# One-hot rows of a routing matrix, built by two engines in place of one

## The chip, the cores and the metric

The kernel runs on one core of a Trainium2 chip. The metric is the device time of one execution in microseconds (us). The profiler's record of one execution is the source of every row shown here; its engines are PE (TensorE matmuls), PEld (its weight loads), DVE (VectorE), ACT (ScalarE), POOL (GpSimd) and SP (SyncE, which issues the weight stream's transfers). A "q" behind an engine's name marks its instruction queue.

## The reference, cut to what matters

One layer of a streaming encoder is computed for 640 tokens: projections, two attentions, a merge, and then PEER, a product-key lookup over 128 x 128 experts. Only PEER touches the change:

```python
v1, i1 = lax.top_k(s1, PEER_TOPK)
v2, i2 = lax.top_k(s2, PEER_TOPK)
...
experts = e1 * PEER_KEYS + e2
gate = jax.nn.softmax(sc, axis=-1)
...
act = jax.nn.gelu(jnp.einsum('nhkd,nd->nhk', u, xt))
w = (gate * act).astype(xt.dtype)
return jnp.einsum('nhk,nhkd->nd', w, v)
```

Each token has 128 picks (8 heads x 16), each with a first key e1, a second key e2 and a gate.

## The kernel before

For 384 of the 640 tokens the kernel doesn't gather expert rows. It computes all 128 x 128 expert activations densely, and multiplies them with a gate matrix G[e1, e2] of each token. G is a product of two 128 x 128 matrices of a token, both with one row per pick: `oh1` has the gate at column e1, `oh2` has a 1 at column e2. So each token costs VectorE two rows-tiles and TensorE one 128 x 128 x 128 product.

The stage that makes G is three loops that run beside each other, one per engine. Each has six trips (the variable `i`) of 16 sets (the variable `q`), and a set is four tokens, so there are 96 sets. In this text set n is the n-th of them, from 0.

- TensorE (L679 to L693) runs two k-steps of an expert unit (L639, six matmuls of 384 columns), waits for `oh_ready` and for `g_evac`, and then makes the four products of the set (L691) into one of two PSUM banks.
- VectorE (L1393 to L1402) waits until the products of the set two before are done (`g_full`), and makes the set's eight tiles, two `tensor_scalar` for each token: L1399 for `oh2`, L1400 for `oh1` with its gate. There are two sets of buffers.
- ScalarE (L1001 to L1014) waits for the products, and copies the bank into a staging buffer (L1007, the evacuation). After sets 7 and 15 of a trip it issues a store of 2 MB to DRAM (L1011), in 512-byte pieces. After the evacuations of sets 8 and 15 it also applies Gelu to an expert unit (L978) and issues a store of that unit (L980). Everything stands in one in-order queue.
- GpSimd splits the next unit's fp32 weights into a high and a low part as soon as TensorE is done with a unit, which is once in 8 sets: one `tensor_scalar` of 2048 columns (L362) and four `tensor_tensor` of 512 (L366). Ten such bursts fall into the 96 sets: the last trip has none.

The rows of the set are `fp32` in SBUF. `iota` is a constant tile with 0 to 127 in each row, `pick_t[0]`, `[1]` and `[2]` hold gate, e1 and e2 with one column per token. Behind the stage ScalarE waits for its stores, and a long stage of expert groups follows.

Of the kernel before, what the change touches and what calls it, by code (L numbers as in the profile page):

```python
# [6 lines left out]
P = 128  # L7
# [12 lines left out]
PH, TOPK, KEYS = 8, 16, 128  # L20
# [6 lines left out]
GT = 32  # L27
GBLK = N2 // GT
# [83 lines left out]
def build(nc, x_t, wstream, u_rows, v_rows, cka, cva, ckb, cvb, rext, negs, bp_b, bs_b, sinks, lnp, lnrow, subk, consts, pt_out, y_out, n_out):  # L112
    f32, f32r, u32 = mybir.dt.float32, mybir.dt.float32r, mybir.dt.uint32
    ALU, ACT = mybir.AluOpType, mybir.ActivationFunctionType
    AX = mybir.AxisListType
    ds = bass.ds

    with ExitStack() as ctx:
# [6 lines left out]
        def sem(name):  # L125
            return ctx.enter_context(nc.semaphore(name))
# [29 lines left out]
        ident, ones, iota, bmask = (cst[:, P * i:P * i + P] for i in range(4))  # L156
# [34 lines left out]
        pick_t = [W2[:, N2 * (q + 2):N2 * (q + 3)] for q in range(3)]  # L191
        oh1 = W2[:, 5 * N2:5 * N2 + 8 * P].rearrange("p (n e) -> p n e", n=8)
# [8 lines left out]
        oh2 = m1_hi[:, 2 * EG * N2:2 * EG * N2 + 8 * P].rearrange("p (n e) -> p n e", n=8)  # L201
# [24 lines left out]
        def acc(s, h):  # L226

            return banks[:, 2 * s + h, 0:WAVES[h][1]]

        def cut(ap, h):  # L230

            return ap[:, WAVES[h][0]:WAVES[h][0] + WAVES[h][1]]
# [11 lines left out]
        def sc_parts(s):  # L244

            return banks[:, 4 + 2 * s, :], banks[:, 5 + 2 * s, 0:P]
# [34 lines left out]
        gexp_in, gexp_done, picks_done, picks_full, picks_taken = (  # L281
            sem(n) for n in ("gexp_in", "gexp_done", "picks_done", "picks_full", "picks_taken"))

        oh_ready, g_full, g_evac = sem("oh_ready"), sem("g_full"), sem("g_evac")
        act_stored = [sem(f"act_stored{s}") for s in range(2)]
        act_in = [sem(f"act_in{e}") for e in range(EG)]
# [163 lines left out]
        def _(pe):  # L450
# [4 lines left out]
            def k_step(s, k, dst, k_first, k_last, phase):  # L455

                if phase is not None and k % 2 == 0:
                    pe.wait_ge(mv_ready, KT_N * phase + k + 2)
                for n, (a, b) in enumerate(((w_hi, mv_hi), (w_hi, mv_lo), (w_lo, mv_hi))):
                    for h in range(2):  # L460
                        last = pe.matmul(acc(dst, h), a[s][:, P * k:P * k + P], b[h][:, k, :],  # L461
                                         start=(k == k_first and n == 0), stop=(k == k_last and n == 2))
                return last
# [121 lines left out]
            with pe.Fori(0, N_PROJ // 2) as i:  # L585
                for s in range(2):
                    m = 2 * i + s
                    pe.wait_ge(split_done, U_PROJ + m + 1)
                    for z in range(2):
                        pe.wait_ge(z_taken, 2 * m + z + 1)  # L590
                        for k in range(8 * z, 8 * z + 8):
                            last = k_step(s, k, z, 8 * z, 8 * z + 7, 1)
# [32 lines left out]
            with pe.Fori(0, N_QUERY // 2) as i:  # L625
# [3 lines left out]
                for k in range(KT_N):  # L629
                    last = k_step(1, k, 1, 0, KT_N - 1, 3)  # L630
# [5 lines left out]
            def act_step(s, k, bank):  # L636

                for n, (a, b) in enumerate(((w_hi, mv_hi), (w_hi, mv_lo), (w_lo, mv_hi))):
                    last = pe.matmul(banks[:, bank, 0:N2], a[s][:, P * k:P * k + P], b[1][:, k, :],  # L639
                                     start=(k == 0 and n == 0), stop=(k == KT_N - 1 and n == 2))  # L640
                if k == KT_N - 1:
                    last.then_inc(unit_done, 1)
                return last
# [23 lines left out]
            for q, src in enumerate((pick_g, pick_e[0], pick_e[1])):  # L667
                for b in range(N2 // P):
                    last = pe.transpose(banks[:, 4 + q, P * b:P * b + P], src[:, 2 + b, :], ident)
# [9 lines left out]
            with pe.Fori(0, GBLK // 2) as i:  # L679
                for q in range(2 * GT // 4):  # L680
                    for k in (2 * q, 2 * q + 1):
                        s, n = k // KT_N, TAIL + 2 * i + k // KT_N
                        if k % KT_N == 0:
                            pe.wait_ge(split_done, U_PEER + n + 1)
                            pe.wait_ge(gelu_done, n - 1)
                        act_step(s, k % KT_N, s)
                    pe.wait_ge(oh_ready, 16 * i + q + 1)
                    pe.wait_ge(g_evac, 16 * i + q + 1)
                    for t in range(4):
                        n = 4 * (q % 2) + t  # L690
                        last = pe.matmul(banks[:, 2 + q % 2, P * t:P * t + P], oh2[:, n, :].bitcast(f32), oh1[:, n, :],  # L691
                                         start=True, stop=True)
                    last.then_inc(g_full, 1)  # L693
# [65 lines left out]
        def _(act):  # L759
# [204 lines left out]
            with act.Fori(0, N_QUERY // 2) as i:  # L964
                for s in range(2):
# [5 lines left out]
                    four, one = sc_parts(s)  # L971
# [3 lines left out]
            def early_activation(n, s, trip):  # L975
                act.wait_ge(unit_done, U_PEER + n + 1)
                act.wait_ge(act_stored[s], 16 * trip)
                act.activation(act_t[s], banks[:, s, 0:N2], ACT.Gelu).then_inc(gelu_done, 1)  # L978
                act.wait_ge(gelu_done, n + 1)
                act.dma_start(a_s[ds(n, 1)].rearrange("a p t -> p (a t)"), act_t[s]).then_inc(act_stored[s], 16)  # L980
# [17 lines left out]


            act.sem_inc(g_evac, 2)  # L1000
            with act.Fori(0, GBLK // 2) as i:  # L1001
                for q in range(2 * GT // 4):
                    w, qq = q // 8, q % 8
                    act.wait_ge(g_full, 16 * i + q + 3)
                    if qq == 0:
                        act.wait_ge(g_stored[w], 16 + 16 * i)
                    act.activation(g_buf[w][:, :, 4 * qq:4 * qq + 4],  # L1007
                                   banks[:, 2 + q % 2, :].rearrange("p (t e) -> p e t", t=4), ACT.Copy).then_inc(g_evac, 1)
                    if qq == 7:
                        act.wait_ge(g_evac, 16 * i + q + 3)  # L1010
                        act.dma_start(G_s[:, :, ds(2 * i + w, 1), :, :].rearrange("g p a e t -> p g (a e t)"),  # L1011
                                      g_buf[w].rearrange("p (g e) t -> p g (e t)", e=EG)).then_inc(g_stored[w], 16)
                    if q in (8, 15):
                        early_activation(TAIL + 2 * i + q // 15, q // 15, TAIL // 2 + i)  # L1014


            for w in range(2):
                act.wait_ge(g_stored[w], 16 + 16 * (GBLK // 2))
# [78 lines left out]
            for i in range(EARLY):  # L1097
                first, q, k = U_LATE + 12 * i, 2 * i + 1, 12 * i
# [35 lines left out]
        def _(dve):  # L1134
# [73 lines left out]
            for mix in "ab":  # L1208
                with dve.Fori(0, PAIRS) as j:
                    own.enter(j, 2 + NS * (1 if mix == "a" else 3))  # L1210
                    dve.wait_ge(att_q, Q_BASE[mix] + Q_PER[mix] * j + Q_PER[mix])
                    for hh in range(2):
                        rows = slice(HD * hh, HD * hh + HD)
                        last = dve.tensor_copy(q_both[rows, :, hh, :],
                                               q_t[rows, 0:P].rearrange("p (b t) -> p b t", b=DEC_B))
# [14 lines left out]
            with dve.Fori(0, N_PROJ // 2) as i:  # L1230
                for s in range(2):
# [4 lines left out]
                    for h in range(2):  # L1236
                        last = dve.tensor_tensor(cut(ga, h), acc(0, h), cut(ga, h), ALU.mult)
                    last.then_inc(z_taken, 1)
                    dve.wait_ge(unit_done, U_PROJ + m + 1)
                    for h in range(2):  # L1240
                        last = dve.tensor_tensor(cut(gb, h), acc(1, h), cut(gb, h), ALU.mult)
# [7 lines left out]
            with dve.Fori(0, N_OUT // 2) as i:  # L1249
                for s in range(2):  # L1250
# [4 lines left out]
                    for h in range(2):  # L1255
                        last = dve.scalar_tensor_tensor(R[:, ds(T * m + WAVES[h][0], WAVES[h][1])], cut(x_res[s], h), ALPHA,
                                                        acc(s, h), ALU.mult, ALU.add)
# [120 lines left out]
            for b in range(2):  # L1378
                dve.tensor_copy(gate_n[b], pick_g[:, b, :])
                for z in range(2):  # L1380
                    at = PICKS * (2 * b + z)
                    last = dve.scalar_tensor_tensor(idx_all[:, at:at + PICKS], pick_e[0][:, b, :], float(KEYS), pick_e[1][:, b, :],
                                                    ALU.mult, ALU.add)
# [9 lines left out]
            with dve.Fori(0, GBLK // 2) as i:  # L1393
                for q in range(2 * GT // 4):
                    dve.wait_ge(g_full, 16 * i + q + 1)
                    for t in range(4):
                        n = 4 * (q % 2) + t
                        tok = ds(2 * GT * i + 4 * q + t, 1)
                        dve.tensor_scalar(oh2[:, n, :], iota, pick_t[2][:, tok], None, ALU.is_equal)  # L1399
                        last = dve.tensor_scalar(oh1[:, n, :], iota, pick_t[1][:, tok], pick_t[0][:, tok],  # L1400
                                                 ALU.is_equal, ALU.mult)
                    last.then_inc(oh_ready, 1)  # L1402


            dve.wait_ge(g_full, 2 + N2 // 4)
# [120 lines left out]
            for i in range(EARLY):  # L1526
                q, first, k = 2 * i + 1, U_LATE + 12 * i + EG, 12 * i
# [120 lines left out]
```

## Time and profile before

| | |
|---|---|
| median of 3 runs | 4622.53 us (4618.06 to 4627.13) |
| the profiled execution's own time | 4623.17 us |
| its span, first to last instruction | 4621.4 us |
| TensorE matmul busy share of the span | 93% |
| the stage that makes G | first L691 at 2224.6 us, last group of L691 at about 2459 us |
| mean granted TensorE clock | 0.976 of full speed |

TensorE is busy nearly everywhere, so time is lost or won where it stands idle. Busy time of overlapping instructions is counted once in a sum, while the mean of one instruction has its whole duration, so that two in a row can start closer together than one lasts.

### The profile page before, as it was taken

What the parts mean: (1) busy time and instruction counts of PE and PEld (TensorE: products, weight loads), DVE (VectorE), ACT (ScalarE), POOL (GpSimd) and SP (SyncE); (2) the same over time, 40 slices, a digit from 0 to 9 for tenths busy, and PEclk for the clock granted to TensorE, in tenths of its full rate; (3) what the DMA queues carried; (4) which work ended last, traced back from release to release, by engine and by line L of the source; (5) the groups of instructions that cost most, each with busy time, mean ns of one, the idle gap of its engine ahead of it and who ended that gap; (6) DMA issues with size and microseconds to landing.
All of it is one profiled execution on the core that took longest, in us unless ns stands there. A gap on an engine that the chain in (4) does not pass through costs nothing.

```text
span 4621.4 us, 71896 instructions
## 1 busy us (share of the span) xinstructions
PE 4310.1 (93%) x26508; PEld 4132.5 (89%) x26508; DVE 2676.7 (58%) x4808; ACT 1060.7 (23%) x1861; POOL 2581.3 (56%) x1653
## 2 busy tenths in 40 slices
PE   8999999999989998985888999999999999999997
PEld 8999888888889997985878999999999999999996
DVE  1000233334432323899796777787777777787776
ACT  1000122222221101100223222322323223223223
POOL 4445332222235453443335777787877878778783
PEclk9999999999999999997999999999999999999998
DMA  5222322222233221111457999999999999999994
GB/s 197 102 98 98 119 103 109 100 92 74 78 135 123 101 96 66 55 65 57 155 157 274 377 391 389 394 405 411 397 384 380 391 385 405 392 403 403 392 418 195
DMA packets 268537, 1082.02 MB, mean 234 GB/s; under 512 B 24496, under 2 KB 89136, under 8 KB 185264
## 3 DMA queue, kind: packets, MB, share of 16 engines
q0 software_dynamic: 74736, 544.24, 28.8%
q1 hardware_dynamic: 87840, 388.01, 22.5%
q10 hardware_dynamic: 105888, 148.96, 9.6%
q8 instruction: 25, 0.41, 0.0%
q14 instruction: 48, 0.39, 0.0%
HBM read 1019.65 MB, written 66.85 MB: 235 GB/s over the span
## 4 chain that ended last, share of the span: by engine, by line
PE 59%; DVE 12%; POOL 11%; DMA 8%; issue 7%; ACT 1%; ACTq 1%; DVEq 0%; POOLq 0%
PE banks L461 29%; PE banks L703 11%; PE banks L639 10%; POOL w_lo L356 8%; DMA work<-in_u_rows,idx_all 3%; POOL work L384 2%; DMA work<-in_v_rows,idx_all 2%; PE banks L530 2%; PE banks L691 2%; PE banks L492 2%; DMA rows_own<-in_u_rows,idx_all 1%; PE banks L500 1%; POOL rows_own L384 1%; DVE work L1312 1%; DMA work<-out_p 1%
## 5 line engine op out<-in xcount | busy, mean ns | idle before, releaser
L356 POOL TENSOR_TENSOR w_lo<-w_raw,w_hi 128x1024 fp32r<-128x1024 f32 x480 | 1153.1, 2403 | 385.5 <-ACT w_hi L1024 374.8
L362 POOL TENSOR_SCALAR w_hi<-w_raw 128x2048 fp32r<-128x2048 f32 x130 | 252.5, 1942 | 1480.3 <-PE banks L461 1273.9
L461 PE MATMUL banks<-mv_hi,w_hi 128*128 128x256 f32 x3648 | 864.2, 318 | 62.3 <-DVE mv_lo L1146 37.4
L461 PE MATMUL banks<-mv_lo,w_hi 128*128 128x256 f32 x3648 | 837.2, 311 | 0.0
L461 PE MATMUL banks<-mv_hi,w_lo 128*128 128x256 f32 x3648 | 836.3, 310 | 0.0
L703 PE MATMUL banks<-mv_hi,w_hi 128*128 128x384 f32 x2048 | 696.9, 340 | 78.4 <-DVE work L1439 61.4
L461 PEld LDWEIGHTS banks<-mv_hi,w_hi 128*128 128x128 f32 x3648 | 652.7, 190 | 126.2 <-issue 102.5
L1024 ACT ACTIVATE w_hi<-w_raw 128x1024 fp32r<-128x1024 f32 x480 | 508.6, 1060 | 982.2 <-PE banks L703 647.9
L639 PE MATMUL banks<-mv_hi,w_hi 128*128 128x384 f32 x2048 | 696.4, 340 | 17.6 <-POOL w_lo L356 13.9
L703 PE MATMUL banks<-mv_lo,w_hi 128*128 128x384 f32 x2048 | 690.6, 337 | 0.0
L703 PE MATMUL banks<-mv_hi,w_lo 128*128 128x384 f32 x2048 | 690.6, 337 | 0.0
L639 PE MATMUL banks<-mv_lo,w_hi 128*128 128x384 f32 x2048 | 687.7, 336 | 0.0
L639 PE MATMUL banks<-mv_hi,w_lo 128*128 128x384 f32 x2048 | 687.7, 336 | 0.0
L366 POOL TENSOR_TENSOR w_lo<-w_raw,w_hi 128x512 fp32r<-128x512 f32 x520 | 681.1, 1341 | 10.8
L461 PEld LDWEIGHTS banks<-mv_lo,w_hi 128*128 128x128 f32 x3648 | 670.2, 190 | 0.0
L461 PEld LDWEIGHTS banks<-mv_hi,w_lo 128*128 128x128 f32 x3648 | 670.1, 190 | 0.0
L1419 DVE SCALAR_TENSOR_TENSOR banks<-work,subkt,banks 128x2048 f32<-128x2048 f32 x192 | 451.8, 2353 | 106.3 <-DMA work<-in_v_rows,idx_all 105.1
L1416 DVE CUSTOM_DVE_ANT_0 work<-work,banks 128x2048 f32<-128x2048 f32 x192 | 438.3, 2285 | 126.9 <-DMA work<-in_u_rows,idx_all 124.5
L703 PEld LDWEIGHTS banks<-mv_hi,w_hi 128*128 128x128 f32 x2048 | 389.0, 190 | 96.1 <-DVE work L1439 72.7
L639 PEld LDWEIGHTS banks<-mv_hi,w_hi 128*128 128x128 f32 x2048 | 387.6, 189 | 18.4 <-issue 14.1
L703 PEld LDWEIGHTS banks<-mv_lo,w_hi 128*128 128x128 f32 x2048 | 389.4, 190 | 0.0
L703 PEld LDWEIGHTS banks<-mv_hi,w_lo 128*128 128x128 f32 x2048 | 389.2, 190 | 0.0
(155 smaller groups left out, 4784.6 us busy)
## 6 DMA issues: line engine op xcount, KB each, us to landing
w_raw<-in_wstream SPq DMA_DIRECT2D x480, 512.0 KB
w_raw<-in_wstream SPq DMA_DIRECT2D x130, 1024.0 KB, 4.8
gate_matrix<-work ACTq DMA_DIRECT2D x12, 2048.0 KB, 9.2
work<-gate_matrix ACTq DMA_DIRECT2D x32, 768.0 KB
out_p<-work ACTq DMA_DIRECT2D x34, 320.0 KB, 2.2
work<-out_p ACTq DMA_DIRECT2D x34, 320.0 KB, 3.4
gate_scratch<-work ACTq DMA_DIRECT2D x32, 320.0 KB, 2.2
work<-gate_scratch ACTq DMA_DIRECT2D x16, 640.0 KB, 3.9
```

The source lines that it names most:

```text
L356: pool.tensor_tensor(w_lo[s][:, part], raw[s][:, part], w_hi[s][:, part].bitcast(f32), ALU.subtract) \
L362: pool.tensor_scalar(w_hi[s][:, :], raw[s][:, :], 1.0, 0.0, ALU.mult, ALU.add).then_inc(hi_done, 1)
L366: last = pool.tensor_tensor(w_lo[s][:, part], raw[s][:, part], w_hi[s][:, part].bitcast(f32), ALU.subtract)
L384: pool.indirect_dma_start(rows_t[n % ROWS], None, (u_rows, v_rows)[pick // PICKS % 2], bass.IndirectOffsetOnAxis(ap=idx_all[:, pick:pick + ...
L461: last = pe.matmul(acc(dst, h), a[s][:, P * k:P * k + P], b[h][:, k, :], start=(k == k_first and n == 0), stop=(k == k_last and n == 2))
L492: last = pe.matmul(bank[:, 0:w], q_t[rows, end - P:end], k_t[rows, end - w:end], start=True, stop=True)
L530: last = pe.matmul(o, v_nat[:, P * kb + HD * hh:P * kb + HD * hh + HD], pt[:, P * c:P * c + P], start=(c == 0), stop=(c == nk - 1))
L639: last = pe.matmul(banks[:, bank, 0:N2], a[s][:, P * k:P * k + P], b[1][:, k, :], start=(k == 0 and n == 0), stop=(k == KT_N - 1 and n == 2))
L703: last = pe.matmul(banks[:, d, 0:N2], a[v % 2][:, at:at + P], b[z][:, e, :], start=(e == 0 and n == 0), stop=(e == EG - 1 and n == 2))
L1024: act.activation(w_hi[s][:, HALVES[h]], raw[s][:, HALVES[h]], ACT.Copy).then_inc(hi_late, 1)
L1416: ins = dve.tensor_tensor_reduce(rows, rows, nat, 1.0, 0.0, ALU.mult, ALU.add, act_n[:, pick % PICKS:pick % PICKS + 1])
L1419: ins = dve.scalar_tensor_tensor(nat, rows, act_n[:, pick % PICKS:pick % PICKS + 1], nat, ALU.mult, ALU.add)
```

## The change

VectorE no longer makes eight tiles of 128 columns for a set. It makes two tiles of 512 columns, each by one `tensor_tensor` that compares a broadcast of `iota` with a broadcast of four columns of picks. Both are plain one-hot rows. `oh1` comes first and raises the new semaphore `oh_equal`, `oh2` raises `oh_ready` as before. ScalarE then multiplies each of the four `oh1` tiles in place by the token's gate column (`gate_rows`, four ACTIVATE with a scale from SBUF), and raises `oh_gated`, for which TensorE now also waits. In ScalarE's queue `gate_rows` of set q + 1 stands ahead of the evacuation of set q. The last of the six trips is written out of the loop, since it has no next set at its end.

```diff
@@ TensorE
                     pe.wait_ge(oh_ready, 16 * i + q + 1)
+                    pe.wait_ge(oh_gated, 16 * i + q + 1)
                     pe.wait_ge(g_evac, 16 * i + q + 1)
@@ ScalarE
             act.sem_inc(g_evac, 2)
-            with act.Fori(0, GBLK // 2) as i:
+
+            def gate_rows(i, q):
+
+                act.wait_ge(oh_equal, 16 * i + q + 1)
+                for t in range(4):
+                    row = oh1[:, 4 * (q % 2) + t, :]
+                    last = act.activation(row, row, ACT.Copy, scale=pick_t[0][:, ds(2 * GT * i + 4 * q + t, 1)])
+                last.then_inc(oh_gated, 1)
+
+            def gate_trip(i, final):
                 for q in range(2 * GT // 4):
                     w, qq = q // 8, q % 8
+                    if q < 2 * GT // 4 - 1 or not final:
+                        gate_rows(i, q + 1)
                     act.wait_ge(g_full, 16 * i + q + 3)
...
+            gate_rows(0, 0)
+            with act.Fori(0, GBLK // 2 - 1) as i:
+                gate_trip(i, False)
+            gate_trip(GBLK // 2 - 1, True)
@@ VectorE
                     dve.wait_ge(g_full, 16 * i + q + 1)
-                    for t in range(4):
-                        n = 4 * (q % 2) + t
-                        tok = ds(2 * GT * i + 4 * q + t, 1)
-                        dve.tensor_scalar(oh2[:, n, :], iota, pick_t[2][:, tok], None, ALU.is_equal)
-                        last = dve.tensor_scalar(oh1[:, n, :], iota, pick_t[1][:, tok], pick_t[0][:, tok],
-                                                 ALU.is_equal, ALU.mult)
-                    last.then_inc(oh_ready, 1)
+                    four = [P, 4, KEYS]
+                    at = slice(4 * (q % 2), 4 * (q % 2) + 4)
+                    keys = iota.unsqueeze(1).to_broadcast(four)
+                    one, two = (p[:, ds(2 * GT * i + 4 * q, 4)].unsqueeze(2).to_broadcast(four) for p in pick_t[1:])
+                    dve.tensor_tensor(oh1[:, at, :], keys, one, ALU.is_equal).then_inc(oh_equal, 1)
+                    dve.tensor_tensor(oh2[:, at, :], keys, two, ALU.is_equal).then_inc(oh_ready, 1)
```

## Rows read from the trace of the kernel before

**Rows 1.** The page's head.

```profile
span 4621.4 us, 71896 instructions
```

**Rows 2.** Waits of the stage: engine and line, for whom, us, times, longest.

```profile
PE banks L691 <- DVE work L1400: 39.0, 21, 2.6
```

**Rows 3.** Timeline of TensorE: start, length, line; in brackets idle time and its releaser.

```profile
2238.22 1.05 PE L691 MATMUL banks<-work,mv_hi 128*128 128x128 f32 x8
...
2242.28 1.70 PE L691 MATMUL banks<-work,mv_hi 128*128 128x128 f32 x8 [1.97 <-DVE work L1400]
...
2247.31 1.16 PE L691 MATMUL banks<-work,mv_hi 128*128 128x128 f32 x8 [1.41 <-DVE work L1400]
...
2249.35 1.05 PE L691 MATMUL banks<-work,mv_hi 128*128 128x128 f32 x8
...
2257.08 1.05 PE L691 MATMUL banks<-work,mv_hi 128*128 128x128 f32 x8
...
2259.01 1.05 PE L691 MATMUL banks<-work,mv_hi 128*128 128x128 f32 x8
...
2262.84 1.16 PE L691 MATMUL banks<-work,mv_hi 128*128 128x128 f32 x8 [1.72 <-DVE work L1400]
...
2267.69 1.16 PE L691 MATMUL banks<-work,mv_hi 128*128 128x128 f32 x8 [2.63 <-DVE work L1400]
...
2448.73 1.05 PE L691 MATMUL banks<-work,mv_hi 128*128 128x128 f32 x8
...
2451.40 1.13 PE L691 MATMUL banks<-work,mv_hi 128*128 128x128 f32 x8 [0.57 <-ACT work L1007]
```

**Rows 4.** Two stretches of eight sets: busy us of PE, PEld, DVE, ACT, POOL; clock.

```profile
2240.80:2261.50 20.70, 17.42 (x112) 16.60 (x112) 20.62 (x65) 5.21 (x10) 7.14 (x6) 0.92 0.53 162
2261.50:2282.00 20.50, 16.02 (x112) 15.37 (x112) 20.44 (x66) 5.24 (x9) 6.97 (x6) 1.00 0.54 163
```

**Rows 5.** Timeline of VectorE inside a burst of GpSimd, and free of one.

```profile
2240.79 1.44 DVE L1400 TENSOR_SCALAR work<-cst,work 128x128 f32<-128x128 f32 x1
...
2249.18 0.34 DVE L1400 TENSOR_SCALAR work<-cst,work 128x128 f32<-128x128 f32 x1
...
2249.63 0.35 DVE L1400 TENSOR_SCALAR work<-cst,work 128x128 f32<-128x128 f32 x1
```

**Rows 6.** Timeline of GpSimd: the four subtractions of the same burst.

```profile
2240.88 5.13 POOL L366 TENSOR_TENSOR w_lo<-w_raw,w_hi 128x512 fp32r<-128x512 f32 x4
```

**Rows 7.** Timeline of ScalarE and its queue, first and last trips.

```profile
2240.09 0.41 ACTq L1011 DMA_DIRECT2D gate_matrix<-work  x1
...
2245.16 0.79 ACTq L980 DMA_DIRECT2D early_act<-work  x1
...
2260.88 0.39 ACTq L1011 DMA_DIRECT2D gate_matrix<-work  x1
...
2262.11 4.56 ACTq L980 DMA_DIRECT2D early_act<-work  x1
2267.20 0.60 ACT L1007 ACTIVATE work<-banks 128x512 f32<-128x512 f32 x1 [5.25 <-issue]
...
2447.10 3.45 ACTq L980 DMA_DIRECT2D early_act<-work  x1
```

**Rows 8.** VectorE's `tensor_tensor` in another stage: min, median and max in ns.

```profile
L1352 DVE TENSOR_TENSOR work<-work,cst x16: 1491/1493/3220, 1905.2 to 2185.1; 128x1280 f32<-128x1280 f32 x16
```

**Rows 9.** Groups by shape: times run, busy us in total, mean ns.

```profile
L1272 DVE TENSOR_TENSOR work<-work 128x384 f32<-128x384 f32 x16 | 7.6, 552 | 0.0
```

**Rows 10.** Timeline of VectorE: a 1280-wide `tensor_tensor` inside a burst of GpSimd.

```profile
2144.01 2.46 DVE L1356 TENSOR_TENSOR work<-work 128x1280 f32<-128x1280 f32 x1
```

**Rows 11.** ScalarE with an operand from SBUF, by shape, and two in a row.

```profile
L956 ACT ACTIVATE mv_hi<-work,lnt 128x384 fp32r<-128x384 f32 x16 | 9.6, 600 | 0.0
L956 ACT ACTIVATE mv_hi<-work,lnt 128x256 fp32r<-128x256 f32 x16 | 8.1, 508 | 15.3 <-DVE work L1286 15.3
...
1839.39 1.01 ACT L956 ACTIVATE mv_hi<-work,lnt 128x256 fp32r<-128x256 f32 x2 [0.97 <-DVE work L1286]
```

More of the change, by code:

```diff
@@ L282, in build @@
             sem(n) for n in ("gexp_in", "gexp_done", "picks_done", "picks_full", "picks_taken"))
+        oh_equal, oh_gated = sem("oh_equal"), sem("oh_gated")
         oh_ready, g_full, g_evac = sem("oh_ready"), sem("g_full"), sem("g_evac")
```

## The prediction

> **What bounds the kernel now.** I read the page first, then the waits of the stage that makes G, then the timelines of each engine around two bursts of GpSimd. TensorE sets the end of the stage, so only its idle time counts. The waits of the stage give that idle time to one cause, VectorE's last tile of a set: 39.0 us in 21 waits [rows 2]. The change is made to that line, so the question is where this time lies, and what stands behind it.
>
> The timeline of TensorE answers the first part. Free of trouble, the products of two sets start 1.93 us apart (2257.08, 2259.01) [rows 3], and VectorE makes one token's pair of tiles in 0.45 us (2249.18 to 2249.63) [rows 5], so 1.81 us a set: it just keeps up. All the idle time stands behind the bursts of GpSimd, where one VectorE tile takes 1.44 us and not 0.34 [rows 5] while GpSimd subtracts in four steps of 1.28 us (5.13 / 4) [rows 6]. Every small VectorE instruction waits for one instruction of GpSimd. In the first half of a trip set 7 starts at 2238.22, set 8 at 2242.28, set 9 at 2247.31 and set 10 at 2249.35: 11.13 us for three sets, where 3 x 1.93 = 5.79 would do, so 5.3 us are lost. In the second half set 15 starts at 2259.01 and set 17 at 2267.69: 8.68 us in place of 3.86, so 4.8 us are lost [rows 3]. Five trips have both bursts. That is 10.1 us a trip, 51 us in all, and the most that a cure could give.
>
> ScalarE's queue answers the second part. It issues the 2 MB store at 2260.88, and the next store's issue starts at 2262.11 and lasts 4.56 us, until 2266.67; the following evacuation starts only at 2267.20, after 5.25 us whose end the profile names "issue" [rows 7]. In the first half the same: store at 2240.09, the next issue ends at 2245.16 + 0.79 = 2245.95. In the last trip it ends at 2447.10 + 3.45 = 2450.55. In the first two the queue comes free 5.8 us after the big store's issue, whatever else goes on. Today that is nearly free, since an evacuation may be a set late: it cost TensorE 0.57 us in one place [rows 3].
>
> **The change, part by part.**
>
> *VectorE's tiles.* A 1280-wide `tensor_tensor` takes 1.49 us [rows 8], a 384-wide one 0.55 [rows 9], so one of 512 takes 0.55 + 128 x (1.49 - 0.55) / 896 = 0.69 us. In a row they start closer: 7.6 / 16 = 0.475 for 384 [rows 9], so 0.61 for 512. A set costs 1.2 us in place of 1.81. Free of a burst that is hidden either way. Inside one, the 1280-wide instruction takes 2.46 us in place of 1.49 [rows 10], 0.97 of waiting; two tiles then cost 2 x (0.61 + 0.97) = 3.2 us a set, where eight waits of about 1.28 would be 10.3. After set 7 (2238.22), with GpSimd's first instruction done at 2240.88, the tiles of sets 9 and 10 are ready at 2241.6, 2243.1, 2244.7 and 2246.3. VectorE's cost thus falls to about a third, and were it alone, most of the first half's loss would go. The other bound, that these instructions don't collide at all, would make it vanish; rows 10 speak against that. The Trainium skill ("SBUF — State Buffer", section "SBUF: two separate sides") calls the port pair of the two engines an exclusive lock, held for the full instruction, and counts a VectorE instruction with two SBUF inputs in. By that page each tile would wait the full 1.28 us, and set 10 would be ready at about 2247.2, an estimate; this trace shows 0.97.
>
> *ScalarE's gates.* The trace has no ACTIVATE of 128 x 128 from SBUF with a scale from SBUF. The nearest has a bias from SBUF: 600 ns at 384, 508 at 256 [rows 11], so 0.42 at 128. Two in a row (256 and 384) take 1.01, where their lengths sum to 1.11, so they overlap by 0.10 and four gates take 3 x 0.32 + 0.42 = 1.35 us. Bounds: 0.9 (the overlap larger) and 1.7 (no overlap, which a changing register offset could bring). With the evacuation (0.60 - 0.10) a set costs ScalarE 4 x 0.32 + 0.50 = 1.78 us, plus its waits; TensorE's pace is 1.93. It fits, barely.
>
> *The new wait.* `gate_rows` of the next set stands behind the slow store issue, and TensorE waits for it. This is where the change puts a stall in place of the one that it removes. I take ScalarE's times from rows 7, plus 0.1 us for the hand-over to TensorE.
> - First half: the queue is free at 2245.95, the gates of set 10 are ready at 2247.4 with the hand-over, so set 10 starts there and not at 2249.35: 1.9 us earlier. Five times: -9.5.
> - Second half: behind the issue comes the loop's end, after which ScalarE started at 2267.20. The gates of set 17 are done at 2268.55, and it starts at 2268.65, not at 2267.69: 1.0 later. Five times: +4.8.
> - Last trip: no burst, but the store stays. The queue is free at 2450.55, so set 10 of that trip starts at 2452.0 and not at 2448.73, set 11 at 2453.9 and not at 2451.40: +2.5.
> - Start: 0.69 + 1.35 + 0.2 in place of 4 x 0.45 + 0.1: +0.3.
>
> Sum: -1.9 us. TensorE's extra wait costs nothing while its queue runs ahead of the matmuls, as in the gapless sets; a cost of 0.03 us would make 3 us.
>
> *The clock.* Behind the 1.97 us of idle time in the first half the products took 1.70 us and not 1.05 [rows 3], and that stretch has a mean granted clock of 0.92, its neighbour 1.00 [rows 4]: TensorE ran partly at the lower level (1.2 GHz). Before, that hid under the second wait (1.41 us). After, TensorE comes from 3 us of idle time (set 10) and from 4.8 to 5.7 us in one piece (set 17), and runs on without a wait: a set at the lower level costs up to 1.9 us more, by the products' ratio (1.70 / 1.05) 1.2. I take 1.5. None of ten places gives 0, all ten 15; half of them, my choice, since one of the two stretches in rows 4 showed it: +7.5.
>
> Together +5.6 us on the profiled execution (span 4621.4 [rows 1], own time 4623.17), which is 0.6 above the median. So 4622.5 + 5.6 = 4628 us. GpSimd's bursts grow by five VectorE tiles, about 2 us, of the 15 between bursts: hidden. Everything behind the stage shifts with it.
>
> **The rivals.**
> 1. *ScalarE sets the pace in every set.* If a gate costs 0.42 us in its turn (no overlap), a set costs 4 x 0.42 + 0.5 = 2.2 us against 1.93: 0.25 x 96 = 24 us, partly in place of the catching up, so +20 to +45: 4650. For it: only 0.15 us of slack a set, and four register offsets. Against: rows 11 show the overlap.
> 2. *The relief wins; it decides if the queue comes free earlier, by 1.5 us or more at each of eleven places.* VectorE's third of the cost then shows: TensorE would lose some 3 us a burst in place of 5, -15 to -20: 4605. For it: rows 2 put all idle time on VectorE. Against: the 5.8 us of rows 7 hold in both halves.
> 3. *The clock falls at nearly every place, or the hand-overs cost 0.3 us more each:* +10 to +20: 4637.
> 4. *No measurable change*, because one held engine replaces the other: this is the forecast itself, -2 to +9.
>
> **How the numbers follow.** About 0.2% (9.2 us) is what a measurement of this kernel can tell from none. Forecast 0.46, rival 3 0.24, rival 1 0.14, rival 2 0.16. The likeliest case gives 4628 (its own range 4620 to 4632). The range leaves out the far halves of rivals 1 and 2 (together some 0.17): 4610 to 4651. Faster by over 0.2%: 0.15 (rival 2 but for its mild end). Same: the forecast, 0.46. Slower: rivals 1 and 3 and the rest of the forecast's upper end, 0.39.
>
> **What would show it.** After the change TensorE's waits before L691 should name ScalarE, not VectorE: about 3 us in the first half and 5 to 6 in the second of each trip, some 45 us in all, no less than before. VectorE's `tensor_tensor` should take 0.69 us free and about 1.6 in a burst, GpSimd's four subtractions 6.5 us or more, the four gates 1.35 us. The stage should run as long as now, 2222 to 2460, within 10 us. I am wrong if a set free of bursts takes over 1.93 us (rival 1), or if the issue behind the big store no longer ends 5.8 us after it (rival 2), or if the idle time keeps VectorE's name.

## The result, and the profile after

The changed kernel takes 4638.96 us (median of 8 runs, 4629.74 to 4642.84) against 4624.12 us (8 runs, 4618.06 to 4629.59) for the kernel before, on the same chip. The ratio is 1.0026, with a 95% interval from 1.0014 to 1.0037: slower by a quarter of a per cent. The profiled execution took 4634.8 us. Its head and engine totals:

```profile
span 4633.0 us, 71424 instructions
...
PE 4315.4 (93%) x26508; PEld 4139.8 (89%) x26508; DVE 2615.2 (56%) x4232; ACT 1172.8 (25%) x2245; POOL 2597.9 (56%) x1653
```

The waits of TensorE in the stage that makes G (2215 to 2475), which answer to [rows 2]:

```profile
PE banks L693 <- issue: 44.4, 11, 5.8
PE banks L693 <- DVE mv_hi L1418: 4.7, 6, 1.6
```

The idle time is 49.1 us where it was 39.0, and only 4.7 us of it still have VectorE's name. The other 44.4 us come in 11 pieces, two in each of five trips and one in the last, under "issue", by which the profile means a wait with no releaser that it can show. L693 is the line of a set's products (L691 before). The timelines tell what is late. TensorE, which answers to [rows 3]:

```profile
2234.52 1.05 PE L693 MATMUL banks<-work,mv_hi 128*128 128x128 f32 x8
2236.46 1.05 PE L693 MATMUL banks<-work,mv_hi 128*128 128x128 f32 x8
2239.18 1.16 PE L693 MATMUL banks<-work,mv_hi 128*128 128x128 f32 x8 [0.62 <-DVE mv_hi L1418]
2243.95 1.13 PE L693 MATMUL banks<-work,mv_hi 128*128 128x128 f32 x8 [2.56 <-issue]
2245.98 1.05 PE L693 MATMUL banks<-work,mv_hi 128*128 128x128 f32 x8
...
2253.71 1.05 PE L693 MATMUL banks<-work,mv_hi 128*128 128x128 f32 x8
2255.64 1.05 PE L693 MATMUL banks<-work,mv_hi 128*128 128x128 f32 x8
2263.50 2.04 PE L693 MATMUL banks<-work,mv_hi 128*128 128x128 f32 x8 [5.76 <-issue]
2267.27 1.91 PE L693 MATMUL banks<-work,mv_hi 128*128 128x128 f32 x8
2270.34 1.05 PE L693 MATMUL banks<-work,mv_hi 128*128 128x128 f32 x8
...
2459.09 1.13 PE L693 MATMUL banks<-work,mv_hi 128*128 128x128 f32 x8 [3.00 <-issue]
```

ScalarE and its queue in the same stretch, which answer to [rows 7] (L1009 are the gates, L1020 the evacuation, L1024 the 2 MB store, L982 the store behind it):

```profile
2236.56 0.41 ACTq L1024 DMA_DIRECT2D gate_matrix<-work  x1
2237.56 1.28 ACT L1009 ACTIVATE work<-work 128x128 f32<-128x128 f32 x4 [1.19 <-DVE work L1417]
...
2239.86 2.57 ACTq L982 DMA_DIRECT2D early_act<-work  x1
2242.57 1.28 ACT L1009 ACTIVATE work<-work 128x128 f32<-128x128 f32 x4 [2.88 <-issue]
...
2255.75 0.40 ACTq L1024 DMA_DIRECT2D gate_matrix<-work  x1
...
2256.97 4.59 ACTq L982 DMA_DIRECT2D early_act<-work  x1
2262.13 1.28 ACT L1009 ACTIVATE work<-work 128x128 f32<-128x128 f32 x4 [5.32 <-issue]
```

The two are read side by side. The second store's issue ends at 2239.86 + 2.57 = 2242.43, 5.9 us after the big store's issue at 2236.56, and in the second half at 2261.56, 5.8 us after 2255.75. The gates of set 10 run from 2242.57 to 2243.85, and set 10 starts on TensorE at 2243.95. The gates of set 17 run from 2262.13 to 2263.41, and set 17 starts at 2263.50. Each of these long pieces ends with the gates behind ScalarE's queue, which the store holds. The short piece ahead of set 9 (0.62 us) is still VectorE's.

VectorE and GpSimd in the same burst, which answer to [rows 5, 6]:

```profile
2239.05 1.75 DVE L1417 TENSOR_TENSOR work<-cst,work 128x512 f32<-128x512 f32 x1
2240.73 1.77 DVE L1418 TENSOR_TENSOR mv_hi<-cst,work 128x512 fp32r<-128x512 f32 x1
...
2247.18 0.69 DVE L1417 TENSOR_TENSOR work<-cst,work 128x512 f32<-128x512 f32 x1 [0.66 <-PE banks L693]
```

```profile
2236.98 6.65 POOL L367 TENSOR_TENSOR w_lo<-w_raw,w_hi 128x512 fp32r<-128x512 f32 x4
```

A tile of 512 takes 0.69 us free and 1.75 us in a burst, and GpSimd's four subtractions take 6.65 us, not 5.13. VectorE's tiles for set 10 are ready at 2240.80 and 2242.50. The gates, which need only the first, start right behind the held queue at 2242.57 and end at 2243.85, so the queue was last here, by some 1.3 us of the 2.56. Without it the second tile would still have held TensorE until about 2242.6. In the second half set 17's tiles are ready at 2258.3 and the queue is free at 2261.6, so there the queue alone sets the end of the wait.

Two stretches of all engines, which answer to [rows 4] (busy us of PE, PEld, DVE, ACT and POOL, then the granted clock): free of slow products, and behind the long wait.

```profile
2240.00:2255.00 15.00, 12.44 (x91) 12.15 (x90) 11.34 (x15) 11.69 (x35) 4.53 (x4) 1.00 0.59 178
2262.00:2270.00 8.00, 6.50 (x27) 6.53 (x27) 1.97 (x4) 5.40 (x15) 0.75 (x1) 0.57 0.74 227
```

With 1.00 as 2.4 GHz, 0.57 is mostly the lower level, 1.2 GHz. There the products of a set take 2.04 and 1.91 us, not 1.05, and the sets behind 17 start 3.77 and 3.07 us apart, not 1.93.

From its first to its last set the stage takes 247.9 us (2220.90 to 2468.84); before it took 234.7 (2224.56 to 2459.22). The stage starts 3.7 us sooner and what follows takes 2.0 us more, which leaves 11.6 us in the span. (The medians differ by 14.8 us: the profiled execution was 4 us faster than its kernel's median.) Over the stage the mean granted clock is 0.92, where it was 0.96.

### The profile page after: what moved, and what is told of

It reads as the page before. It is cut to its first block, busy times and chain, and to the rows that moved or that the text cites. A ratio compares the mean times of both kernels' runs of the same rounds, so it can differ in the third digit from the quotient of the medians.

```text
span 4633.0 us, 71424 instructions
## 1 busy us (share of the span) xinstructions
PE 4315.4 (93%) x26508; PEld 4139.8 (89%) x26508; DVE 2615.2 (56%) x4232; ACT 1172.8 (25%) x2245; POOL 2597.9 (56%) x1653
## 4 chain that ended last, share of the span: by engine, by line
PE 60%; DVE 12%; POOL 10%; DMA 9%; issue 8%; ACT 1%; ACTq 0%; DVEq 0%; POOLq 0%
PE banks L462 30%; PE banks L640 11%; PE banks L705 11%; POOL w_lo L357 7%; DMA work<-in_u_rows,idx_all 3%; DMA work<-in_v_rows,idx_all 3%; POOL work L385 2%; PE banks L693 2%; PE banks L531 2%; PE banks L493 1%; DVE banks L1435 1%; PE banks L501 1%; DVE work L1329 1%; DVE work L1337 1%; DMA rows_own<-in_u_rows,idx_all 1%
## 5 line engine op out<-in xcount | busy, mean ns | idle before, releaser
L363 POOL TENSOR_SCALAR w_hi<-w_raw 128x2048 fp32r<-128x2048 f32 x130 | 252.2, 1940 | 1469.9 <-PE banks L462 1270.2
L367 POOL TENSOR_TENSOR w_lo<-w_raw,w_hi 128x512 fp32r<-128x512 f32 x520 | 697.3, 1371 | 10.9
```

The lines of the kernel that those rows point to most:

```text
L363: pool.tensor_scalar(w_hi[s][:, :], raw[s][:, :], 1.0, 0.0, ALU.mult, ALU.add).then_inc(hi_done, 1)
L367: last = pool.tensor_tensor(w_lo[s][:, part], raw[s][:, part], w_hi[s][:, part].bitcast(f32), ALU.subtract)
```

## The experiments

Unless said otherwise, an edit is made to the changed kernel, ratios are against the kernel before on the same chip, and "stage" is the time from the first set's products to the last's. At 1.935 us a set, 95 intervals would take 183.8 us. The kernel before itself had medians of 4625.0, 4631.2 and 4623.4 us in three groups of experiments (the first four runs; both runs with fillers of the first size and the first two with fine pieces; the rest), so times of different groups are compared by their ratios.

### The stores behind the big one, moved by three sets

```diff
-                    if q in (8, 15):
-                        early_activation(TAIL + 2 * i + q // 15, q // 15, TAIL // 2 + i)
+                    if q == 3 and not first:
+                        early_activation(TAIL + 2 * i - 1, 1, TAIL // 2 + i - 1)
+                    if q == 11:
+                        early_activation(TAIL + 2 * i, 0, TAIL // 2 + i)
```

The last one follows behind the loop. Nothing is left out.

> The changed kernel, but the Gelu of a finished unit and the issue of its store stand three sets later in ScalarE's queue (behind set 11, and behind set 3 of the next trip), when the 2 MB store in front of it has been taken up. Theory 1 (the gates are held behind that issue): no wait of TensorE of over 2 us that ends with the gates, no slow clock behind them; what is left are some 3.3 us a burst of GpSimd, so the stage takes 184 + 10 x 3.3 + 2 = 219 us against 247.9 (changed) and 234.7 (before): 4608 us, 0.3% faster than before. Theory 2 (four gates a set are too much for ScalarE, wherever the stores stand): stage of 240 us or more, no faster than the changed kernel by over 5 us.

Measured: 4613.65 us (9 runs), ratio 0.9968 [0.9956, 0.9979]; stage 224.0 us. TensorE's waits, and the moved store's issue:

```profile
PE banks L693 <- DVE mv_hi L1422: 28.2, 31, 1.6
...
PE banks L693 <- issue: 2.5, 8, 0.3
```

```profile
2252.76 0.34 ACTq L982 DMA_DIRECT2D early_act<-work  x1
```

The issue takes 0.34 us and holds nobody. The long waits are gone, and with them every slow product: the granted clock is 1.00 over the whole stage. The same change of the tiles that costs 0.26% behind the held queue gains 0.32% without it. The stage comes out 5 us longer than I expected: VectorE in a burst still costs 4.0 us (the intervals 2.70, 3.36, 3.13, 2.04, 2.43 sum to 13.66, five free ones to 9.67).

The same move in the kernel before:

> The kernel before with the same move of Gelu and store, and nothing else. Theory 1: in the kernel before the queue's hold is hidden behind VectorE, so only the 0.6 us of the last trip are won: same as before within 2 us. If instead the hold costs the kernel before as well (rival), it is 5 us or more faster.

Measured: 4622.35 us (12 runs), ratio 0.9997 [0.9987, 1.0008]; stage 233.8. As expected: in this kernel the hold costs nothing that can be told, in the changed one, where TensorE's inputs go through ScalarE, it costs 24 us of stage.

### One part of the change alone

Only `oh2` is made wide, and `oh1` stays a gated tile of VectorE's, with no work for ScalarE:

```diff
+                    dve.tensor_tensor(oh2[:, at, :], iota.unsqueeze(1).to_broadcast(four), two, ALU.is_equal)
                     for t in range(4):
...
-                        dve.tensor_scalar(oh2[:, n, :], iota, pick_t[2][:, tok], None, ALU.is_equal)
                         last = dve.tensor_scalar(oh1[:, n, :], iota, pick_t[1][:, tok], pick_t[0][:, tok],
```

> One part alone: oh2 by one 512-wide comparison, oh1 by four tensor_scalar with the gate on VectorE as before; ScalarE unchanged. Theory 1: VectorE takes the port five times a set in place of eight, and nothing is held: 0.5 to 1 us less a burst, so 5 to 10 us faster than before. Rival (the wide instruction costs more in a burst than it saves, since it also holds GpSimd): same or slower than before.

Measured: 4638.86 us (8 runs), ratio 1.0027 [1.0016, 1.0037]; stage 251.5. A miss, and the most useful run. It has fewer instructions that wait for GpSimd, yet is as slow as the full change. Its waits of TensorE, TensorE's timeline, and the tiles that it waits for:

```profile
PE banks L691 <- DVE work L1403: 40.9, 21, 3.4
```

```profile
2258.40 1.16 PE L691 MATMUL banks<-work,mv_hi 128*128 128x128 f32 x8 [0.58 <-DVE work L1403]
2263.99 2.07 PE L691 MATMUL banks<-work,mv_hi 128*128 128x128 f32 x8 [3.35 <-DVE work L1403]
2267.78 1.91 PE L691 MATMUL banks<-work,mv_hi 128*128 128x128 f32 x8
2270.63 1.05 PE L691 MATMUL banks<-work,mv_hi 128*128 128x128 f32 x8
```

```profile
2237.39 4.97 DVE L1403 TENSOR_SCALAR work<-cst,work 128x128 f32<-128x128 f32 x4
```

The idle time is that of before, 40.9 us against 39.0 [rows 2], and the stage is 16.8 us longer. What differs is the shape: 0.58 and 3.35 us, where before it was 1.72 and 2.63 [rows 3]. Behind the longer piece the products run at 2.07 and 1.91 us, and the intervals 3.79 and 2.85 lose 2.8 us. Four narrow tiles in a row, 4.97 us, all meet GpSimd and delay one set. The same happens behind all ten late sets of the stage (the five in the first halves lose 1.7 us each), and its mean granted clock is 0.90, where it was 0.96. This made the clock, not the sum of the waits, the suspect.

Only the gates are moved, and the tiles stay narrow:

```diff
+                    for rows, pick, done in ((oh1, pick_t[1], oh_equal), (oh2, pick_t[2], oh_ready)):
+                        for t in range(4):
+                            tok = ds(2 * GT * i + 4 * q + t, 1)
+                            last = dve.tensor_scalar(rows[:, 4 * (q % 2) + t, :], iota, pick[:, tok], None, ALU.is_equal)
+                        last.then_inc(done, 1)
```

> The other part alone: the gates on ScalarE as in the changed kernel, but the one-hot tiles still by eight tensor_scalar of 128 columns. Theory 1: pays the hold and the slow clock in the second half of a trip, and keeps VectorE's loss in the first half (10.9 us from set 7 to set 10 in place of 9.4), so about 7 us slower than the changed kernel, 20 us slower than before. Rival (wide tiles bring nothing here, the whole loss is the move of the gates): same as the changed kernel.

Measured: 4654.54 us (5 runs), ratio 1.006 [1.0047, 1.0073]; stage 266.7. Moving the gates alone costs 30 us, where I expected 20; the wide tiles give half of it back. The clock has a part in it: all eleven long pieces of the stage (3.2 to 5.2 us) are followed by slow products, where the expectation had only those of the second halves, and the mean granted clock is 0.87. Free sets still start 1.93 us apart, so ScalarE's work fits in the pace.

### Is it the clock? Products that fill the wait

TensorE computes products of two constants into the bank that the set's own products overwrite, at the place where it waits longest (set 17, the set behind the loop's turn). The wait for the free bank is put ahead of them. No output changes; the idle time becomes work.

```diff
+                    for t in range(fillers.get(q, 0)):
+                        pe.matmul(banks[:, 2 + q % 2, P * (t % 4):P * (t % 4) + P], ident, iota, start=True, stop=True)
                     pe.wait_ge(oh_ready, 16 * i + q + 1)
```

With 44 of them at q = 1 of trips two to six, and, in the kernel with the wide `oh2` alone, 26 ahead of each burst's late set (sets 9 and 17):

> The changed kernel, with 44 products of two constant tiles (128 x 128 x 128, 0.11 us each, 4.9 us in all, written to the bank that the set's own products then overwrite) ahead of TensorE's wait for the gates of set 1 of trips 1 to 5, where it stands idle for 5.8 us. The hold stays as it is. Theory 1 (the sets behind the hold are slow because of TensorE's lower clock, which the idle time brings): sets 18 and 19 follow at 1.9 us and not at 3.8 and 3.1, which takes 10 to 13 us off the changed kernel. Rival (they are slow because VectorE and ScalarE have to catch up): no change, or some us slower.

> The kernel with only oh2 made wide, with 26 such products (2.9 us) ahead of the wait of set 9 (trips 0 to 4) and of set 1 (trips 1 to 5), where it idles for 3.4 us in one piece. If that kernel lost its time to the clock alone, since its idle time is that of the kernel before (40.9 and 39.0 us), this one takes back 15 to 20 us and comes out within 5 us of the kernel before. If the wide instruction itself costs the time, it stays 13 us slower than before.

Measured: 4645.58 us (7 runs), ratio 1.0036 [1.0022, 1.0050], stage 257.9; and 4641.95 us (10 runs), 1.0026 [1.0015, 1.0037], stage 252.2. Both were sized wrongly. I took one product for one matmul record, but the trace of the first shows two for each, and so 9.99 us for 44, which outlasts the 5.8 us wait:

```profile
2256.90 9.99 PE L690 MATMUL banks<-cst 128*128 128x128 f32 x88
2266.72 1.06 PE L695 MATMUL banks<-work,mv_hi 128*128 128x128 f32 x8
2268.66 1.05 PE L695 MATMUL banks<-work,mv_hi 128*128 128x128 f32 x8
```

The times thus decide nothing, but the sets behind now start 1.94 us apart, at 1.06 and 1.05 us. In their proper sizes, 22 and 13:

> The changed kernel with 22 filler products and not 44: one product of fp32 tiles turned out to take 0.22 us (two passes), so 22 last 4.9 us and end inside the hold. Theory (the clock): set 17 starts 7.9 us after set 16 as in the changed kernel, sets 18 and 19 follow at 1.9 us and not at 3.8 and 3.0; 5 x 2.3 us in the mean, so 8 to 13 us faster than the changed kernel, stage of 236 to 240 us. Rival (backlog): no gain.

> The kernel with only oh2 wide, with 13 filler products (2.9 us) in each of the ten places. Theory (the clock): sets 10 and 11 follow at 1.9 us and not at 3.7 and 2.9, so the stage takes 251.5 - 5 x 1.7 - 5 x 2.8 = 229 us, and the kernel is 3 to 8 us faster than before. Rival (the wide instruction itself): stays slower than before.

The first, in the changed kernel: 4631.22 us (11 runs), ratio 1.0018 [1.0010, 1.0027]; stage 241.2, 6.7 us shorter. I expected 8 to 13 us and a stage of 236 to 240. By the ratios the gain is 0.08%, and the two intervals overlap, so the evidence here is the timeline and not the time. Its TensorE:

```profile
2259.42 5.07 PE L690 MATMUL banks<-cst 128*128 128x128 f32 x44
2266.20 1.13 PE L695 MATMUL banks<-work,mv_hi 128*128 128x128 f32 x8 [1.71 <-ACT work L1015]
2268.21 1.05 PE L695 MATMUL banks<-work,mv_hi 128*128 128x128 f32 x8
```

Four of the five intervals up to set 17 are 7.87 to 8.00 us, as without fillers (7.81 to 7.94), the fifth 8.72. The two behind it sum to 3.96 on average and not to 6.15. That is 10.9 us less behind set 17. Slow products are left behind three of the six unfilled waits of the first halves, where the changed kernel had them behind one; those and the interval of 8.72 take 4 us of it back.

The second, with `oh2` alone: 4622.43 us (12 runs), ratio 0.9999 [0.9990, 1.0008]; stage 230.3, 21 us shorter than the same kernel without fillers. The late sets' intervals are 4.9 to 5.5 us, 5.59 without fillers (2258.40 to 2263.99 above), and the next 1.9 to 2.1, not 3.79. Its time is equal to the kernel before's, where I expected 3 to 8 us less. The engine that bounds the stage does more work, and the stage is 21 us shorter. The granted clock over the stage, the last number but two of each row, says why. Without the fillers and with them:

```profile
2220.60:2473.00 252.40, 212.21 (x1338) 205.44 (x1338) 217.17 (x475) 61.48 (x106) 76.50 (x52) 0.90 0.51 158
```

```profile
2227.50:2459.00 231.50, 218.90 (x1598) 213.96 (x1598) 216.18 (x475) 61.63 (x107) 76.53 (x52) 1.00 0.56 172
```

At 1.00 TensorE never left the upper level in this stage. That leaves no room for the rival that the wide instruction itself costs the time: it is still there, and VectorE's busy time is all but the same (217.2 and 216.2 us).

### GpSimd in finer pieces

GpSimd splits each tile in 4 copies of 512 columns and 8 subtractions of 256, not 1 and 4:

```diff
-                pool.tensor_scalar(w_hi[s][:, :], raw[s][:, :], 1.0, 0.0, ALU.mult, ALU.add).then_inc(hi_done, 1)
...
                 for c in range(4):
                     part = slice(D // 4 * c, D // 4 * c + D // 4)
+                    last = pool.tensor_scalar(w_hi[s][:, part], raw[s][:, part], 1.0, 0.0, ALU.mult, ALU.add)
+                last.then_inc(hi_done, 1)
+                pool.wait_ge(hi_done, 2 * pair + s + 1)
+                for c in range(8):
+                    part = slice(D // 8 * c, D // 8 * c + D // 8)
```

Together with the moved stores, then in the kernel before, then in the changed kernel with its stores where they were:

> The changed kernel with the late stores, and GpSimd's split in 4 + 8 pieces of 512 and 256 columns in place of 1 + 4 of 2048 and 512. If what is left (4 us a burst) is one wait for one GpSimd instruction per tile, then shorter instructions take most of it: 1 to 2 us a burst, stage of 200 to 208 us against 224, 15 to 20 us faster than with the late stores alone. If the burst simply gets longer (more instructions, each with VectorE's tile in between), within 5 us of it.

> The kernel before with GpSimd's split in the same finer pieces and nothing else. Every small tile of VectorE then waits 0.6 us and not 1.3, but still eight of them make a set: 12 tiles in a burst in place of 5. Some 1 us less a burst, 8 to 12 us faster than before; if the pieces' own overhead counts elsewhere in the kernel, no faster.

> The changed kernel with GpSimd's split in 4 + 8 pieces and the stores where the change left them. The hold of ScalarE's queue doesn't depend on GpSimd: 9.8 us from set 15 to set 17 and the slow clock behind it stay, 9.3 from set 7 to set 10 too, so the stage takes 240 to 248 us; the 24 us that the pieces give ahead of the stage remain: about 4612 us, against 4562 with both. If the pieces alone cured the stage, it would come to 4575.

The first: 4562.48 us (4 runs), ratio 0.9853 [0.9833, 0.9873]; stage 199.1. GpSimd and VectorE inside a burst, and TensorE's waits in the stage:

```profile
2235.64 9.03 POOL L370 TENSOR_TENSOR w_lo<-w_raw,w_hi 128x256 fp32r<-128x256 f32 x8
```

```profile
2238.30 1.22 DVE L1425 TENSOR_TENSOR mv_hi<-cst,work 128x512 fp32r<-128x512 f32 x1
```

```profile
PE banks L696 <- issue: 6.6, 13, 0.6
PE banks L696 <- DVE mv_hi L1425: 2.0, 1, 2.0
```

A tile waits 1.22 - 0.69 = 0.53 us, half of 1.06. Two take 2.3 us, near TensorE's 1.93, and the idle time almost vanishes. The stage also starts 23 us sooner than before (2201.5). VectorE's stages ahead of it meet GpSimd too. One of their groups by shape (times run, busy us, mean ns), in the changed kernel and then in this one:

```profile
L1277 DVE TENSOR_TENSOR work<-work 128x640 f32<-128x640 f32 x16 | 28.2, 1766 | 0.5
```

```profile
L1284 DVE TENSOR_TENSOR work<-work 128x640 f32<-128x640 f32 x16 | 17.0, 1064 | 0.5
```

The kernel before with fine pieces: 4605.92 us (6 runs), ratio 0.9948 [0.9930, 0.9965]. That is 16 to 32 us less, where I expected 8 to 12, but not for the reason that I gave, less waiting in the stage's bursts. The gain is all ahead of the stage (start at 2197.9, 27 us sooner); the stage itself takes 241.3 us, 6.6 more than before, at a mean granted clock of 0.92. A set there:

```profile
2218.43 2.08 PE L694 MATMUL banks<-work,mv_hi 128*128 128x128 f32 x8 [2.63 <-DVE work L1403]
```

A wait of 2.63 us in one piece is followed by 2.08 us of products: here the clock falls too, where the kernel before had passed such a wait at 1.16 [rows 3].

The changed kernel with fine pieces: 4618.57 us (11 runs), ratio 0.9993 [0.9983, 1.0003]; stage 252.9, 5 us longer than the changed kernel's and 5 above the most that I expected. Its first-half waits are single pieces of 3.2 to 3.3 us, where the changed kernel's were 0.6 and 2.4 to 2.6, and four of the five are followed by slow products, not one; the mean granted clock of the stage is 0.90. Its waits:

```profile
PE banks L696 <- issue: 47.8, 11, 5.8
```

So the stage of the changed kernel takes 247.9 us as it is, 224.0 with the stores moved, 252.9 with fine pieces, and 199.1 with both. Fine pieces are worth 25 us there, but only once the queue is free.

Last, 8 copies and 16 subtractions with the moved stores:

> Late stores, and GpSimd's split in 8 + 16 pieces of 256 and 128 columns. If the wait of a tile is that of one GpSimd instruction, it falls from 0.5 to 0.3 us and the stage to about 190 us (199 with 4 + 8 pieces): 5 to 10 us faster than that. If GpSimd's own cost of an instruction counts by now (a burst must end before the next), same or slower than with 4 + 8 pieces.

Measured: 4555.43 us (4 runs), ratio 0.9861 [0.9843, 0.9879]; stage 197.7, where I expected 190. The interval holds the first version's ratio, so whether it is any faster is open. A tile waits only about 0.25 us (0.94 - 0.69), but more often, since GpSimd is now busy for 174 of the stage's 198 us (125 of 200 in the first version):

```profile
2235.85 0.94 DVE L1425 TENSOR_TENSOR mv_hi<-cst,work 128x512 fp32r<-128x512 f32 x1
...
2237.03 0.69 DVE L1424 TENSOR_TENSOR work<-cst,work 128x512 f32<-128x512 f32 x1 [0.25 <-PE banks L696]
```

## Why the prediction was right or wrong

The measured 4639 us lies in the range (4610 to 4651), above the likeliest case's own (4620 to 4632) and next to rival 3 (4637). I gave "no measurable change" the larger chance, and the kernel is slower by just over what can be told. The mechanism is the one forecast; one term, the clock's, was too small. One sign that I named failed: the stage was to run as long as before within 10 us, and it runs 13.3 longer.

- **VectorE's tiles: right.** 0.69 us free as worked out, 1.75 in a burst against 0.61 + 0.97 = 1.58. They start 1.68 us apart, so a set costs 3.4 us, not 3.2. The Trainium skill's rule ("SBUF — State Buffer", section "SBUF: two separate sides", a lock for the whole instruction) would make a tile wait 1.28 us, the length of one subtraction. The wait is 1.06, so the measured exclusion is some 0.2 us shorter than the instruction. With subtractions of 256 columns (0.74 us, the median of that run) the wait is 0.53, again 0.2 less. Which of the two engines' instructions has the part that overlaps, no run shows.
- **The held queue: right.** The queue comes free 5.8 to 5.9 us behind the big store's issue in nine of ten places, in both halves, and 6.2 in the tenth; it is as long with fine pieces, where TensorE still waits up to 5.8 us. The late-store run shows it by its removal: 24 us of stage. Rival 2, which needed an earlier release, is out.
- **ScalarE's gates: right.** Four take 1.28 us against 1.35, and free sets keep 1.93 us. Rival 1 is out. Their group in the stage (times run, busy us, mean ns, and the idle time before them by what ended it):

```profile
L1009 ACT ACTIVATE work<-work 128x128 f32<-128x128 f32 x384 | 122.8, 390 | 71.1 <-issue 44.0 <-DVE work L1417 26.8
```

- **First half: right in kind, -7.6 us measured for -9.5.** Sets 7 to 10 take 9.4 us, against 9.2 worked out. But I took the 11.13 us of the first trip for all; the other four took 10.8, so the gain is 1.5 us a trip.
- **Second half: +5.6 for +4.8; last trip +2.5 for +2.5; start none for +0.3.** Sets 15 to 17 take 9.8 us, not 8.68. In the last trip the wait ahead of 2459.09 makes one interval 5.10 us.
- **The clock: mis-sized, +12.5 for +7.5.** This is the step that fell short. The text took 1.5 us at half of ten places; six paid, 2.1 us each. The sets 17 to 19 take 6.84, 5.64, 5.88, 6.76 and 5.62 us in the five trips, where before they took 3.97: +10.9 us, so all five places behind the long wait pay, 1.7 to 2.9 us each, not 1.5. Of the five first halves one pays, 1.6 us. I let a place cost one set at the lower level; the traces show up to two, because the second set's products still ran at 1.91 us. And I spread the chance evenly over waits of 3 and 5 us, where the longer ones always cost. That the count came out near the chosen half is luck: I took it because one of two stretches in [rows 4] was slow, but in the kernel before the products were slow (1.57 to 1.77 us) behind the first wait (1.8 to 2.0 us) of all five first halves and in no second half, and after the change it is nearly the reverse. Rival 3 had the clock fall at nearly every place, which is also not what came; the price per place was what was off. The fillers show the cause: with the wait filled and set 17 no sooner, the sets behind return to 3.96 us, and in the kernel with `oh2` alone the fillers bring the granted clock of the stage from 0.90 to 1.00.

The terms as measured: -7.6 + 5.6 + 2.5 + 12.5 = 13.0, against 13.3 us by which the stage grew. Without the clock the change would have come out at about zero (+0.5), near what the prediction's other terms say (-1.9), though the halves' two terms were each off, by 1.9 and 0.8 us, both to the slow side.

**Where the expected gain went.** VectorE's relief is real, 24 us of stage once nothing stands behind it; it was given back at once because the gates were put behind an issue that holds ScalarE's queue, and the idle time moved into one long piece, which the clock made longer still. Whether the hold could be avoided by another queue for the second store was not tried.

## What to carry to other kernels

Before an operation is moved to an engine with idle time, look in that engine's queue for instructions that hold it, and move those first: here the same change costs 0.26% behind them and gains 0.32% without them. Waits of TensorE are not worth their sum: look at the longest piece and at the length of the products behind it. Here every piece over 3.3 us cost 1.5 to 2.9 us on top of its own length. Shorter ones did so in part, and in the kernel before the slow products behind the first of two waits cost nothing, since TensorE had to wait again behind them. Where VectorE and GpSimd meet, cut GpSimd's instructions shorter: with the moved stores it made this kernel 1.5% faster than the one before (1.4% in the finest pieces), and 23 of the 60 us by which the profiled span shrank lay ahead of this stage, where nobody had looked.

## What was not expected of the hardware

- Equal idle time cost unequally: 39.0 us in pieces of up to 2.6 us gave a stage of 234.7 us, 40.9 us in pieces of up to 3.4 us one of 251.5. Every unfilled piece over 3.3 us, in all runs, was followed by slow products, up to 1.9 to 2.1 us (granted clock 0.57 in the stretch shown). Shorter ones differ: of six of 2.4 to 3.0 us in the changed kernel one was, of six of 2.5 to 3.0 us in the run with 22 fillers three, of five of 3.2 to 3.3 us in the changed kernel with fine pieces four. In the kernel before, all five of 1.8 to 2.0 us that open a first half's burst were followed by products of 1.57 to 1.77 us, and none of the five of 2.63 us in the second halves; with its stores moved, two of the five that open a burst (1.8 to 2.0 us) were. What tips these is open.
- Work with no use, put in the waits of the kernel with `oh2` alone, gave 21 us of stage back.
- A product of 128x128x128 in this format shows as two matmuls and takes 0.23 us (9.99 / 44).
- The issue of a second store behind the 2 MB one takes 2.4 to 4.9 us in the changed kernel and ends 5.8 to 5.9 us after the first (6.2 once); three sets later it takes 0.34. Why it is slow behind the first, no run shows.
- GpSimd's smaller pieces cost it more themselves: in bursts eight subtractions of 256 take 9.03 us, four of 512 take 6.65.
